# Spreading product-key gates on Trainium2: the first factor made token by token in one compare-and-scale operation, and six of eight tokens of the second factor widened by ScalarE

## The reference

```python
vals, idx = lax.top_k(sc, PEER_TOPK)
cand = vals[:, :, 0, :, None] + vals[:, :, 1, None, :]
best, flat = lax.top_k(cand.reshape(...), PEER_TOPK)
i1 = jnp.take_along_axis(idx[:, :, 0], flat // PEER_TOPK, axis=-1)
i2 = jnp.take_along_axis(idx[:, :, 1], flat % PEER_TOPK, axis=-1)
expert = i1 * PEER_NKEYS + i2
gate = jax.nn.softmax(best, axis=-1)
...
u_sel = u_emb[ec]
act = jax.nn.gelu(jnp.einsum('td,thkd->thk', tc, u_sel), approximate=False)
return jnp.einsum('thk,thkd->td', (act * gc).astype(tc.dtype), v_emb[ec])
```

## Time and profile before

| what | us |
|---|---|
| median of three runs | 3759.49 |
| lowest and highest of the three | 3753.37, 3774.87 |
| the profiled execution, its own time | 3772.18 |
| its span, first to last instruction | 3770.4 |
| VectorE busy | 2324.8 |
| ScalarE busy | 942.6 |
| TensorE busy (matmul) | 3248.3 |
| first start of L1328 to the last start | 1388.7 to 1666.4 |

### The profile page before, as it was taken

The page is one execution under the profiler, slowest core; times in us unless marked ns, Lnnn a source line. Parts: engine busy times, 40 slices in busy tenths (PEclk is TensorE's granted clock), DMA queues, the critical chain, the costliest instruction groups (busy, mean ns, idle before and its releaser), DMA issues. The chain is left out here.

```text
span 3770.4 us, 47531 instructions
## 1 busy us (share of the span) xinstructions
PE 3248.3 (86%) x17309; PEld 2553.0 (68%) x17309; DVE 2324.8 (62%) x5058; ACT 942.6 (25%) x1346; POOL 977.4 (26%) x941
## 2 busy tenths in 40 slices
PE   8997998889676625546999999999999999999995
PEld 4444666664455515536999988888788888888883
DVE  2122334433499999974888877777777777544443
ACT  2212233331111115642222222222122222222221
POOL 0000000000023220001333345555555555222222
PEclk9996578989888869987999999999999999999998
DMA  4113101100200003557777779999999999666655
GB/s 183 47 59 92 25 17 34 45 17 34 94 26 26 13 1 101 167 162 261 252 246 258 247 270 349 351 354 355 346 346 351 351 351 353 243 227 219 219 208 195
DMA packets 326829, 706.22 MB, mean 187 GB/s; under 512 B 72432, under 2 KB 165872, under 8 KB 325104
## 3 DMA queue, kind: packets, MB, share of 16 engines
q0 software_dynamic: 110592, 402.70, 29.5%
q1 hardware_dynamic: 211328, 295.76, 22.6%
q10 hardware_dynamic: 4720, 5.26, 0.4%
HBM read 632.86 MB, written 70.78 MB: 187 GB/s over the span
## 5 line engine op out<-in xcount | busy, mean ns | idle before, releaser
L1548 PE MATMUL psum<-hn_hi_e,u_hi 128*128 128x320 f32 x2048 | 635.1, 310 | 59.1 <-DMA hn_lo_e<-scr_lo 55.5
L1548 PE MATMUL psum<-hn_hi_e,u_lo 128*128 128x320 f32 x2048 | 635.3, 310 | 0.0
L1548 PE MATMUL psum<-hn_lo_e,u_hi 128*128 128x320 f32 x2048 | 635.3, 310 | 0.0
L1532 POOL DMA_INDIRECT v_ring<-v_rows,eidT x384 | 440.7, 1148 | 699.4 <-PE psum L1591 593.4
L1564 PE MATMUL psum<-v_hi,w_hi 128*128 128x512 f32 x1280 | 511.6, 400 | 10.7 <-DVE coefT L1721 8.8
L1698 DVE TENSOR_TENSOR res<-psum,res 128x512 f32<-128x512 f32 x640 | 434.1, 688 | 124.4 <-PE psum L1564 124.4
L1564 PE MATMUL psum<-v_lo,w_hi 128*128 128x512 f32 x1280 | 501.5, 392 | 0.0
L1564 PE MATMUL psum<-v_hi,w_lo 128*128 128x512 f32 x1280 | 500.0, 391 | 0.0
L1525 POOL DMA_INDIRECT res<-u_rows,eid x288 | 339.7, 1179 | 387.4 <-DVE dots L1709 326.8
L1548 PEld LDWEIGHTS psum<-hn_hi_e,u_hi 128*128 128x128 f32 x2048 | 386.8, 189 | 64.7 <-DMA hn_lo_e<-scr_lo 55.7
L1678 DVE TENSOR_TENSOR w<-psum,w 128x640 f32<-128x640 f32 x128 | 105.6, 825 | 482.4 <-ACT psum L1631 482.4
(11 more groups left out here) (226 smaller groups left out, 4770.1 us busy)
## 6 DMA issues: line engine op xcount, KB each, us to landing
u_raw<-uT SPq DMA_DIRECT2D x128, 512.0 KB, 5.7
v_raw<-v_rows SPq DMA_DIRECT2D x128, 512.0 KB, 6.9
scr_g<-gates SPq DMA_DIRECT2D x5, 8192.0 KB, 30.6
w<-scr_g SPq DMA_DIRECT2D x128, 320.0 KB, 4.5
scr_m<-st_m SPq DMA_DIRECT2D x8, 1024.0 KB, 3.8
w_raw<-in_w_pq SPq DMA_DIRECT2D x8, 1024.0 KB, 5.5
w_in<-in_w_in SPq DMA_DIRECT2D x3, 2048.0 KB, 15.5
scr_a<-st_a SPq DMA_DIRECT2D x8, 768.0 KB, 3.2
```

What stands on the lines that cost most here:

```text
L1532: pool.indirect_dma_start(v_ring[:, m % V_RING, :], None, core.i["v_rows"], bass.IndirectOffsetOnAxis(eidT[:, m // P, t:t + 1], 0)).then_i ...
L1548: last = nc.tensor.matmul(ps[:, a, 0:COLS], x[:, c, j, :], y[:, j, a * COLS:(a + 1) * COLS], start=m == 0, stop=m == len(terms) - 1)
```

## The change

The first factor no longer goes through a bf16 table. For each of the 8 tokens, one VectorE `tensor_scalar` reads the f32 table 0 to 127 (`iota_f`), compares it with the token's first key and multiplies by its gate; both are per-partition operands read from `flat`, and the 128 results are written contiguously. `one1` and the first keys' bf16 copy go. `second` is now widened for six tokens by ScalarE and two by VectorE. TensorE waits for 8 counts of `first_ready` per octet.

```diff
-    ON_ACT = 4
+    ON_ACT = 6
...
-        one1 = sb("one1", [P, BUFS, NKEY, OCT], bf16)
...
-        keysT = sb("slot_keys", [P, 2, TD], bf16)
+        keysT = sb("slot_keys", [P, TD], bf16)
...
-            nc.vector.tensor_copy(keysT[:, :, :], flat[:, 0:2, :]).then_inc(keys_ready, 1)
+            nc.vector.tensor_copy(keysT[:, :], flat[:, 1, :]).then_inc(keys_ready, 1)
...
             for n in range(NOCT):
                 b = n % BUFS
                 need(dve, second_act, n - BUFS + 1)
-                need(dve, first_ready, n - BUFS + 1)
                 need(dve, second_dve, n - BUFS + 1)
-                for z, dst in ((0, one1), (1, one2)):
-                    nc.vector.tensor_tensor(
-                        dst[:, b, :, :], iota[:, :, :],
-                        keysT[:, z, n * OCT:(n + 1) * OCT].rearrange("p (o t) -> p o t", o=1)
-                        .to_broadcast([P, NKEY, OCT]), ALU.is_equal).then_inc(ones_ready, 1)
+                nc.vector.tensor_tensor(
+                    one2[:, b, :, :], iota[:, :, :],
+                    keysT[:, n * OCT:(n + 1) * OCT].rearrange("p (o t) -> p o t", o=1)
+                    .to_broadcast([P, NKEY, OCT]), ALU.is_equal).then_inc(ones_ready, 1)
                 need(dve, spread_done, n - BUFS + 1)
-                dve.wait_ge(ones_ready, n * 2 + 1)
-                nc.vector.tensor_tensor(
-                    first[:, b, :, :].rearrange("p t i -> p i t"), one1[:, b, :, :],
-                    flat[:, 2, n * OCT:(n + 1) * OCT].rearrange("p (o t) -> p o t", o=1)
-                    .to_broadcast([P, NKEY, OCT]), ALU.mult).then_inc(first_ready, 1)
-                dve.wait_ge(ones_ready, n * 2 + 2)
+                for t in range(OCT):
+                    at = n * OCT + t
+                    nc.vector.tensor_scalar(first[:, b, t, :], iota_f[:, :], flat[:, 0, at:at + 1], flat[:, 2, at:at + 1],
+                                            ALU.is_equal, ALU.mult).then_inc(first_ready, 1)
+                dve.wait_ge(ones_ready, n + 1)
...
-                pe.wait_ge(first_ready, n + 1)
+                pe.wait_ge(first_ready, (n + 1) * OCT)
...
-                act.wait_ge(ones_ready, n * 2 + 2)
+                act.wait_ge(ones_ready, n + 1)
```

## The result

The changed kernel takes 3714.9 us in the median of 15 runs (3687.78 to 3754.03), the kernel before 3759.49 us in the median of 15 (3732.9 to 3802.65). The ratio is 0.9887, with a 95% interval of 0.9856 to 0.9918: 1.1% faster, 44.6 us by the medians, where 48 were forecast.

What follows compares the result with a forecast made beforehand. VectorE alone was taken to bound the stage: 0.605 + 2.01 + 0.295 = 2.91 us per octet instead of 3.515, times 79, gains 48 us, bringing the median from 3759.49 to 3711.5 us; range 3676 to 3738.

Steps and rivals of the forecast that it cites:

- VectorE alone bounds the stage: In the changed stage, VectorE is busy 140.00 of 140 us and nothing makes it wait; it alone sets the pace.
- The step of 0.251 us for two operands from memory: VectorE's eight small operations per octet: the second operand adds 53 ns again, 0.251 us each, 2.01 us together; chance 0.45.
- its two bounds: VectorE's small operation: 0.198 us with the second operand free (rival, chance 0.33), 0.251 if it adds 53 ns.
- The cast of two tokens, 0.295: VectorE's remaining share of `second` per octet: 0.07 fixed plus 0.225 us, instead of 0.52 for four tokens.
- ScalarE's 1.64 us for 768 elements: ScalarE's widening of six tokens per octet: 206 ns plus 1.86 ns per element, 1.64 us; bounds 1.37 and 1.74.
- The waits among them: Between the stage's engines: nobody holds VectorE, and TensorE's 2.02 us per octet fit in the period of 2.91.
- What follows the stage moves as a whole: Behind the stage: `run_experts` first loads when the last store has landed, 33.4 us later, so the kernel gains the stage's gain.
- The sum, 48 us: Whole stage: octets at 2.91 instead of 3.515 us, times 79, gain 48 us; median 3711.5 us.
- the halved rate: Rival: VectorE operations that compare or have two memory operands take 72 ns longer; period 3.06 to 3.46 us; chance 0.15.
- the lost overlap: Rival: each small VectorE operation begins only when the one before has written; 3764 or 3784 us; chance 0.07.
- The durations near 334 ns: Sign in the changed stage: VectorE's small operations last near 334 ns, against 281 if the second operand is free.

Runs made afterwards that it cites:

- the single edits: Two kernels: the change with ScalarE widening four tokens (ratio 0.9941 to the kernel before), and the kernel before with ScalarE widening six (0.9936).
- the run with four kinds: Changed kernel, first factor made by four kinds of operation, two tokens each: steps 0.255 (two memory operands), 0.195 (one), 0.135 (constants), 0.205 us (multiplying two tensors).
- the run with one operand: Changed kernel with the gate replaced by a constant, so each small operation has one operand from memory: octets 2.47 us apart, steps of 0.195 us.

## Why the prediction was right

Point by point, in its own order:

- *VectorE alone bounds the stage.* Right, before and after: it is busy 110.00 of 110 us, and each of the single edits moved the octets by VectorE's sum alone.
- *The step of 0.251 us for two operands from memory.* Measured 0.256. The choice between its two bounds was what the forecast hung on, and it fell on the right one. The profile before could not settle it, and at chances of 0.45 and 0.33 there was luck in it; the run with four kinds settled it, with 0.06 us for each operand.
- *The cast of two tokens, 0.295, by taking off the 0.07 of an almost empty operation.* Measured 0.30, and 0.18 for one token against 0.185 expected by the same reckoning. It held because 1, 2 and 4 rows are handled alike; the same line through 3 rows would have failed by 0.33 us.
- *ScalarE's 1.64 us for 768 elements.* Measured 1.63, and 1.86 us for 896 elements, where the slope of 1.86 ns per element gives 1.88. ScalarE's sum, forecast at 2.49, came to 2.47 in the run with one operand, where VectorE no longer held it up.
- *The waits among them.* Right but for one wait of 0.4 us in the third octet. TensorE does not start with the octet on VectorE, as assumed, but 0.41 us into it (1561.54 to 1561.95): 0.16 us until the cast's end and 0.25 until the start behind it. This costs nothing, since ScalarE's widening ends only when the matmuls do (1563.96 and 1563.97).
- *What follows the stage moves as a whole.* Right: 2064.7 and 2061.0 us behind it.
- *The sum, 48 us.* The stage gave 45.2 us between the two profiles and the medians 44.6. The term that was too good by 3 us is the eight operations: 8 x 0.005 us x 79. Two things that the sum left out give 0.9 us back: there are 80 octets and not 79 (0.56 us), and the cast of the keys at the start fell from 0.93 to 0.60 us.

Of the rivals, the halved rate and the lost overlap are refuted by the run with four kinds. The small operations last 327 ns and more and follow each other at 0.256 us. The forecast took only half of what the Trainium skill says on this ("VectorE: DVE Perf Modes", section "The DRAIN you can't avoid"): the next operation does not start until the pipe is empty, but, as the section goes on, one that is not held starts earlier. These independent operations, with steps shorter than their durations, agree with the second half. The durations near 334 ns that I named as a sign were there in the second profile of the changed kernel (median 339) and only as the minimum in the first (327, median 360); the steps were the sound sign, not the durations.

## What to carry to other kernels

Price a short operation by its start-to-start step and not by its duration, and add up what it carries: for 128 f32 elements on VectorE it was 0.135 us, and 0.06 more for each per-partition operand. Splitting one operation into eight paid here because the one took 1.80 us for 1024 elements and needed a comparison in front of it (0.605), while eight contiguous ones cost 2.05 together. That the 1.80 us come from its writes with a long stride is not shown, since no run wrote it contiguously. An estimate from the run with four kinds: a contiguous multiplication of two tensors cost 0.205 us for 128 elements, 0.07 of it fixed, so 1024 would take about 1.15 us in one operation, and some 0.65 us go with the layout. When an engine is the only bound of a stage, its edits add up and its neighbours' idle time can be filled one by one, until their sums meet: 2.47 us for ScalarE, 2.31 for GpSimd and 2.49 for VectorE were reached here.

## What the runs showed of the hardware that was not expected

- A cast of three rows costs more than one of four on VectorE: 0.74 against 0.52 us.
- Each per-partition operand adds its own 0.06 us to an operation on VectorE: 0.135, 0.195 and 0.255 us with none, one and two.
- GpSimd takes 0.9 to 1.16 us in the mean for an operation that VectorE does in 0.256, and its single durations lie between 0.78 and 1.62 us; VectorE's own steps grow only from 0.256 to 0.265 beside it, in the mean of six.
- Durations on VectorE differ from one execution to the next (medians from 330 to 479 ns for the same small operation in kernels that issue it eight times in a row) while the steps stay at 0.256 us.
- The clock granted to TensorE in the attention stages was 0.77 in one profile and 0.84 in another, with 35 us between them in a part of the program that the change doesn't touch; at 0.78, in a third, the difference was 2.8 us.
